# A two-block transformer kernel on one core: weight parts split in quarters beside the attentions, and the first output projection in split fp32r products

## The reference, cut to what matters

```python
# block 1
h = layernorm(concat(meta, x))                     # 528 tokens x 1024
o = concat(rmsnorm(MLA heads 0..3), rmsnorm(GQA heads 0..3))
mix = o @ w_o                                      # [512, 1024] x [1024, 1024]
h = layernorm(ALPHA * h + mix)
logits = h @ w_router; top-4 of 32 experts, softmax gates
h = layernorm(ALPHA * h + experts(h))              # 32 experts, clamped SwiGLU
# block 2
q_a, k_a, v_a, q_b, k_b, v_b, gate0, gate1 = h @ w_in_2
a = relative-bias attention, 8 heads of 64;  b = differential attention, 4 heads
h = layernorm(ALPHA * h + (g0 * (a @ w_branch_a) + g1 * (b @ w_branch_b)) @ w_out)
h = layernorm(ALPHA * h + relu(h @ w_ff1)**2 @ w_ff2)
```

## Time and profile before

| | |
|---|---|
| median of 3 runs | 2364.81 us (2363.74 to 2370.38) |
| the profiled execution | 2365.33 us, its span 2363.3 us |
| TensorE busy | 2258.0 us, 96% of the span |
| VectorE busy | 1650.4 us, 70% |
| ScalarE busy | 1208.7 us, 51% |
| mean granted TensorE clock | 0.976 |

### The profile page before, as it was taken

How to read it: one execution, slowest core, us unless ns; L and a number is a source line. 1 busy time by engine, 2 the same in 40 slices (tenths; PEclk the granted TensorE clock), 3 DMA queues, 4 the chain that set the end, 5 groups by cost and what they waited for, 6 DMA issues and landing times.

```text
span 2363.3 us, 29103 instructions
## 1 busy us (share of the span) xinstructions
PE 2258.0 (96%) x10440; PEld 1820.3 (77%) x10440; DVE 1650.4 (70%) x1575; ACT 1208.7 (51%) x1195; POOL 331.7 (14%) x274
## 2 busy tenths in 40 slices
PE   7999969999999999999999999859999999999998
PEld 4668557888888888888888888747676787888886
DVE  3636578999999999999999999742446626432434
ACT  2134325777777777777777777623334522421320
POOL 4042011211111111111211211110210010000000
PEclk9999969999999999999999999979999999999999
DMA  7010148999999999999999999653121133222220
GB/s 270 1 55 22 39 152 339 396 390 382 380 394 375 382 393 375 383 393 376 386 386 378 388 389 375 240 195 107 45 79 37 57 122 117 98 107 100 78 107 36
DMA packets 141297, 550.85 MB, mean 233 GB/s; under 512 B 11456, under 2 KB 12608, under 8 KB 124272
## 3 DMA queue, kind: packets, MB, share of 16 engines
q1 hardware_dynamic: 128048, 505.70, 55.4%
q0 software_dynamic: 11024, 39.98, 6.6%
q10 hardware_dynamic: 2160, 4.28, 0.5%
HBM read 523.71 MB, written 26.21 MB: 233 GB/s over the span
## 4 chain that ended last, share of the span: by engine, by line
PE 78%; DVE 3%; ACT 2%; issue 1%; DMA 1%; POOL 0%; DVEq 0%; ACTq 0%; POOLq 0%
PE PS L365 74%; PE PS L680 1%; PE PS L674 1%; ACT ring_parts L1472 1%; ACT act L1546 0%; DVE act L1660 0%; DVE st L1633 0%; DVE act L1665 0%; PE PS L876 0%; PE PS L790 0%; DVE small L2161 0%; DMA acc_d<-act,to_c 0%; DMA act<-acc_d 0%; DVE ring_parts L2083 0%; DMA act<-h_d,tl_c 0%
## 5 line engine op out<-in xcount | busy, mean ns | idle before, releaser
L365 PE MATMUL PS<-act_parts 128*128 128x512 f32 (+1 forms) x3324 | 1043.0, 394 | 16.3 <-DVE act_parts L1983 7.7
L1832 DVE TENSOR_TENSOR low<-ring,act_parts 128x2048 fp32r<-128x2048 f32 x396 | 886.1, 2290 | 37.1 <-ACT act_parts L1367 37.1
L365 PEld LDWEIGHTS PS<-act_parts 128*128 128x128 f32 x3324 | 625.6, 189 | 145.5 <-issue 15.9
L1367 ACT ACTIVATE act_parts<-ring 128x2048 fp32r<-128x2048 f32 x396 | 729.8, 1913 | 11.9 <-PE PS L365 8.1
L365 PE MATMUL PS<-low,act_parts 128*128 128x512 f32 x1584 | 618.7, 391 | 0.0
L365 PE MATMUL PS<-act_parts,ring_parts 128*128 128x512 f32 (+1 forms) x1280 | 376.2, 385 | 0.3 <-DVE act_parts L2201 0.3
L365 PEld LDWEIGHTS PS<-low,act_parts 128*128 128x128 f32 x1584 | 298.6, 189 | 60.5
L2083 DVE TENSOR_TENSOR ring_parts<-ring,ring_parts 128x4096 fp32r<-128x4096 f32 x30 | 132.7, 4425 | 219.1 <-ACT ring_parts L1472 219.0
L365 PEld LDWEIGHTS PS<-act_parts,ring_parts 128*128 128x128 f32 x1280 | 239.1, 191 | 59.6 <-issue 12.7
L365 PE MATMUL PS<-ring_parts,act_parts 128*128 128x512 f32 x1088 | 261.8, 393 | 2.1 <-DVE act_parts L2233 2.1
L365 PEld LDWEIGHTS PS<-ring_parts,act_parts 128*128 128x128 f32 x1088 | 205.0, 189 | 47.7 <-issue 4.3
(11 more groups left out here) (244 smaller groups left out, 1667.8 us busy)
## 6 DMA issues: line engine op xcount, KB each, us to landing
ring<-w_gate_up SPq DMA_DIRECT2D x264, 1024.0 KB, 8.6
ring<-w_down SPq DMA_DIRECT2D x132, 1024.0 KB, 7.8
ring<-w_ff SPq DMA_DIRECT2D x16, 2048.0 KB, 7.7
ring<-w_in SPq DMA_DIRECT2D x12, 2048.0 KB, 9.8
ring<-w_o SPq DMA_DIRECT2D x1, 4096.0 KB, 24.6
ring<-w_out SPq DMA_DIRECT2D x2, 2048.0 KB, 8.2
acc_d<-ring POOLq DMA_DIRECT2D x5, 512.0 KB, 3.3
act<-x SPq DMA_DIRECT2D x4, 512.0 KB, 5.5
```

Of the source, the lines that this page charges most:

```text
L365: return eng.matmul(o, lhsT, rhs, start=first, stop=last, **kw)
L1367: A_(W1hi[c % CS], W1[c], ACT.Copy).then_inc(sem["high"], 1)
L1832: tt(W1lo[c], W1[c], W1hi[c % CS].bitcast(F32), ALU.subtract).then_inc(sem["low"], 1)
```

## The change

1. In block 2, `split_piece(n, m)` splits a quarter (1024 columns) of a slot. Slots 4, 5, 6 get their quarters in units 0..3, 6..9 and 11..14 of the first attention on ScalarE (one unit later on VectorE), slots 7 and 8 in units 0..3 and 8..11 of the second. The whole-part splits of slots 4 to 8 go.
2. At the seam, the last unit's attend_a(15) moves behind scores_b(0) and beside(24), out_a(15) on ScalarE behind probs_b(0), and VectorE's masked(0) no longer waits for the last output of the first attention. At the end, attend_b(15) takes PSUM bank 6, and take_b(15) stands between two halves of heads_low(0).
3. In block 1, the projection is made from split operands: 192 fp32r matmuls for 64 float32 ones. ScalarE writes high parts of w_o times the gains (eight of 128x1024) and of the transposed heads (eight of 128x512), VectorE the eight low parts of w_o; its `take_heads` subtracts where it multiplied. The new parts lie where chunks 1 to 3 of expert 0 have their high parts, so these three move behind the projection's last matmul, on ScalarE and on VectorE.

```diff
+PIECES = 4
+SPLIT_A = ((4, 0), (5, 6), (6, 11))
+SPLIT_B = ((7, 0), (8, 8))
+WO_AT = (18, 20, 22, 23, 24, 26, 28, 30)
 # TensorE: project(g, t)
                     for k in range(4 * g, 4 * g + 4):
-                        ins = mm(PS[:, b, :], oT[:, k, t * P:(t + 1) * P], w_o_s[:, k, hf * 512:(hf + 1) * 512],
-                                 k == 4 * g, k == 4 * g + 3)
+                        if t == 0 and hf == 0:
+                            eng.wait_ge(*past("wo_low", k + 1))
+                        mm(PS[:, b, :], oThi[:, k, rows], w_o_hi[k][:, cols], k == 4 * g, False)
+                        mm(PS[:, b, :], oThi[:, k, rows], w_o_lo[:, k, cols], False, False)
+                        ins = mm(PS[:, b, :], oTlo[g][:, k - 4 * g, rows], w_o_hi[k][:, cols], False, k == 4 * g + 3)
...
 # TensorE: seam and end
-            for q in range(UA + 2):
+            for q in range(UA + 1):
...
-                if q >= 2:
+                if 2 <= q <= UA:
                     attend_a(q - 2)
...
-                b = next_bank(6)
+                if u == 0:
+                    eng.wait_ge(*past("vb2_out", 4))
+                b = next_bank(6) if u < UB - 1 else 6
...
+                if u == 0:
+                    attend_a(UA - 1)
 # ScalarE: first attentions of block 1
+                if 18 <= u < 22:
+                    turned_heads(0, u - 18)
+                if u in WO_AT:
+                    w_o_high(WO_AT.index(u))
...
-            for c in range(4):
-                chunk_high(0, c, first=True)
+            chunk_high(0, 0, first=True)
...
-            for c in range(4, CS):
+            eng.wait_ge(*past("mix_psum", 16))
+            for c in range(1, CS):
                 chunk_high(0, c, first=True)
 # ScalarE: block 2
+            def split_piece(n, m):
+                cols = slice(m * SW // PIECES, (m + 1) * SW // PIECES)
+                if m == 0:
+                    eng.wait_ge(*past(f"slot{n % NW}_in", 16 * (n // NW + 1)))
+                    eng.wait_ge(*past(*slot_used(n - NH)))
+                A_(W2hi[n % NH][:, cols], W2[n % NW][:, cols], ACT.Copy).then_inc(signal("w_high"), 1)
...
-                split_weights(c + 2)
+                if c == 1:
+                    split_weights(3)
...
-                    if n == 7 or n == 15:
-                        split_weights(5 + n // 8)
-            split_weights(7)
+                for n, at in SPLIT_A:
+                    if at <= q < at + PIECES:
+                        split_piece(n, q - at)
 # VectorE
             def take_heads(g, t):
...
-                tt(oT[:, 4 * g:4 * g + 4, t * P:(t + 1) * P], four(bank_of("oT_psum", n)), gains, ALU.mult).then_inc(
-                    signal("oT_out"), 1)
+                eng.wait_ge(*past("oT_hi", n))
+                tt(oTlo[g][:, :, rows], four(bank_of("oT_psum", n)), oThi[:, 4 * g:4 * g + 4, rows].bitcast(F32),
+                   ALU.subtract).then_inc(signal("oT_out"), 1)
+            def w_o_low(k):
+                eng.wait_ge(*past("wo_high", k + 1))
+                stt(w_o_lo[:, k, :], w_o_s[:, k, :], gq[:, 5 + k:6 + k], w_o_hi[k].bitcast(F32), ALU.mult,
+                    ALU.subtract).then_inc(signal("wo_low"), 1)
...
+                if u - 1 in WO_AT:
+                    w_o_low(WO_AT.index(u - 1))
...
-                else:
-                    chunk_low(0, 2 * t - 4)
-                    chunk_low(0, 2 * t - 3)
+                elif t == 2:
+                    chunk_low(0, 0)
...
+            chunk_low(0, 1)
             rows_low(0)
...
-            for c in range(4, 8):
+            for c in range(2, 8):
                 chunk_low(0, c)
...
-            for n in range(1, 5):
+            for n in range(1, 4):
                 split_weights(n)
...
-                if q in (5, 10):
-                    split_weights(5 + q // 10)
-            split_weights(7)
+                for n, at in SPLIT_A:
+                    if at < q <= at + PIECES:
+                        split_piece(n, q - at - 1)
...
-                if u == 0:
-                    eng.wait_ge(*past("oa_out", 2 * UA))
-                if u >= 2:
-                    eng.wait_ge(*past("expb", 2 * u - 2))
+                eng.wait_ge(*(past("expb", 2 * u - 2) if u >= 2 else past("proba", 2 * (UA - 1 + u))))
...
+                if u == UB:
+                    heads_low(0, range(2))
                 if 1 <= u <= UB:
                     take_b(u - 1)
-                if u == 8:
-                    split_weights(8)
+                for n, at in SPLIT_B:
+                    if at < u <= at + PIECES:
+                        split_piece(n, u - at - 1)
                 if u == UB:
-                    heads_low(0)
+                    heads_low(0, range(2, NT))
```

More of the change, by code:

```diff
@@ L194, in build @@
         w_in_s = ring[:, 0:KD * ZCOLS].rearrange("p (k c) -> p k c", k=KD)
-        oT = ring[:, 8192:8192 + KD * S].rearrange("p (k s) -> p k s", k=KD)
+        oThi = ring_parts[:, 8192:8192 + KD * S].rearrange("p (k s) -> p k s", k=KD)
+        oTlo = [part(9216, 4, S), part(22528, 4, S)]
         wqb = ring[:, 20480:22016].rearrange("p (k c) -> p k c", k=2)
@@ L198, in build @@
         w_o_s = ring[:, 12288:20480].rearrange("p (k c) -> p k c", k=KD)
+        w_o_lo = ring_parts[:, 12288:20480].rearrange("p (k c) -> p k c", k=KD)
+        w_o_hi = [part(at, D) for at in (5120, 6144, 7168, 8192, 14528, 15552, 18368, 19392)]
         H1 = ring[:, 20480:24576].rearrange("p (t d) -> p t d", t=NT)
@@ L592, in project @@
                 eng.wait_ge(*past("oT_out", NT * g + t + 1))
+                rows = slice(t * P, (t + 1) * P)
                 for hf in range(2):
-                    n = 8 * g + 2 * t + hf
+                    n, cols = 8 * g + 2 * t + hf, slice(hf * 512, (hf + 1) * 512)
                     b = next_bank()
@@ L1336, in heads_std, with turned_heads, w_o_high @@
                    bias=EPS_1).then_inc(signal("o_std"), 1)
+            def turned_heads(g, t):
+                n = NT * g + t + 1
+                eng.wait_ge(*past("oT_psum", n))
+                A_(oThi[:, 4 * g:4 * g + 4, t * P:(t + 1) * P], four(bank_of("oT_psum", n)), ACT.Copy).then_inc(
+                    signal("oT_hi"), 1)
+            def w_o_high(k):
+                A_(w_o_hi[k], w_o_s[:, k, :], ACT.Copy, scale=gq[:, 5 + k:6 + k]).then_inc(signal("wo_high"), 1)
             U = (HM + HG) * NT
@@ L1351, in _ @@
             heads_std(1)
+            for t in range(NT):
+                turned_heads(1, t)
             eng.wait_ge(*past("angles", 1))
@@ L1569, in _ @@
                     probs_b(u)
+                if u == 0:
+                    out_a(UA - 1)
+                if u == UB:
+                    heads_high(0)
                 if u >= 2:
                     square_b(u - 2)
-                if u == UB:
-                    heads_high(0)
+                for n, at in SPLIT_B:
+                    if at <= u < at + PIECES:
+                        split_piece(n, u - at)
                 if u < UB and u % 2:
@@ L1796, in take_heads @@
             def take_heads(g, t):
-                n = NT * g + t + 1
-                gains = gq[:, 5 + 4 * g:9 + 4 * g].rearrange("p (j o) -> p j o", o=1).to_broadcast([P, 4, P])
-                eng.wait_ge(*past("oT_psum", n))
-                tt(oT[:, 4 * g:4 * g + 4, t * P:(t + 1) * P], four(bank_of("oT_psum", n)), gains, ALU.mult).then_inc(
-                    signal("oT_out"), 1)
+                n, rows = NT * g + t + 1, slice(t * P, (t + 1) * P)
+                eng.wait_ge(*past("oT_hi", n))
[5 more added lines that the diff above has]
+                    ALU.subtract).then_inc(signal("wo_low"), 1)
             U = (HM + HG) * NT
@@ L2080, in split_weights, with split_piece @@
             def split_weights(n):
-                eng.wait_ge(*past("w_high", n + 1))
-                tt(W2lo[n % NW], W2[n % NW], W2hi[n % NH].bitcast(F32), ALU.subtract).then_inc(signal("w_low"), 1)
+                eng.wait_ge(*past("w_high", PIECES * (n + 1)))
+                tt(W2lo[n % NW], W2[n % NW], W2hi[n % NH].bitcast(F32), ALU.subtract).then_inc(
+                    signal("w_low", PIECES), PIECES)
+            def split_piece(n, m):
+                cols = slice(m * SW // PIECES, (m + 1) * SW // PIECES)
+                eng.wait_ge(*past("w_high", PIECES * n + m + 1))
+                tt(W2lo[n % NW][:, cols], W2[n % NW][:, cols], W2hi[n % NH][:, cols].bitcast(F32), ALU.subtract).then_inc(
+                    signal("w_low"), 1)
             def low(tag, XT, hi, tiles=range(NT)):
@@ L2195, in scale_heads, with heads_low @@
                        ALU.mult).then_inc(signal("ob_out"), 1)
-            def heads_low(g):
-                for t in range(NT):
+            def heads_low(g, tiles=range(NT)):
+                for t in tiles:
                     rows = o2_rows(t, g)
```

17 lines of the change are left out of this document (9 added, 8 removed).

## The result

The changed kernel takes 2340.41 us (median of 4 runs, 2338.53 to 2343.33); the kernel before, run beside it, 2364.89 us (4 runs, 2363.74 to 2370.38). The ratio is 0.9894, 95% interval 0.9882 to 0.9906. The profiled execution took 2340.29 us, its span is 2338.5 us. Forecast were 2338.5 us, range 2330 to 2350.

A forecast was written before the change was run, and what follows sets the result against it. The prediction took TensorE's time (matmuls, idle gaps, slow clock) to bound the kernel. Savings of 6.4 + 6.1 + 1.3 + 8.3 + 4.2 = 26.3 us from 2365.33 gave 2339.0, or 2338.5 against the median; range 2330 to 2350.

The forecast's parts named there:

- Block 2, first attention: Block 2's first attention: TensorE's gaps and slow clock behind them go with quarters; 6.4 + 6.1 + 1.3 us saved.
- The three gaps: TensorE's idle gaps of 4.92, 4.60 and 1.28 us in block 2's first attention, all forecast to go.
- Between the two lies at least one half product: First attention: 2.7 us of half product between VectorE's quarter and the next maximum's scores hides the quarter's 1.2 us.
- Seam, second attention, end: From take_a(15) to branch a in block 2: VectorE's sum rules, its earlier start saves 8.3 us.
- if TensorE's sum ruled, 9.7: Upper bound for seam to branch a: 9.7 us saved if TensorE's work, not VectorE's, set the time.
- TensorE's own sum: Second attention: from scores_b(0) at 1771.4, 4 x 18.11 plus 2.0 and 1.9 us, ending at 1847.7.
- Block 1, matmuls: Block 1's output projection: three fp32r products replace two-record float32 ones, 11.6 us less 1.0, so 10.6 saved.
- the 1.0 us taken off for VectorE: Projection's second half: deduction for jitter of a VectorE-TensorE tie at 8.1 us a tile and VectorE's late last-tile start.
- Block 1, what it adds: Block 1's attention loop: added w_o parts and head copies cost 1.9 us; bounds 0 and 9.8.
- waits for VectorE anyway: Block 1's loop, units 19 and 21 with take_heads: TensorE already waits, so both w_o_low overruns show, 0.9 us.
- Block 1, the moved chunks: Routing behind block 1's projection: ScalarE's five chunk copies delay the gates' exponentials; VectorE waits 4.5 us.
- The rival of the free gates: Block 1's routing: gates don't hold the chain, the 4.5 us come back, total 2334 us; chance 0.12.

The follow-up runs named there:

- e3: Changed kernel with whole parts in place of quarters, VectorE still splitting one unit after ScalarE; 2341.61 us, ratio 0.9880 to the kernel before.
- e12: Changed kernel with VectorE's quarters in the same unit as ScalarE's, not one unit later; 2339.95 us, ratio 0.9887 to the kernel before.
- e7: Changed kernel with whole parts in place of quarters and VectorE's split in the same unit as ScalarE's; 2354.57 us, ratio 0.9954 to the kernel before.
- e6: Changed kernel with VectorE's second-attention quarters between masked(u) and mix_b(u), in its wait for ScalarE, not behind take_b; 2335.76 us, ratio 0.9868.
- e8: Changed kernel with the seam's order undone: attend_a(15), out_a(15) ahead of scores_b(0), masked(0) waiting for the last outputs; 2343.66 us, ratio 0.9907.
- e4: Changed kernel with the gates' exponentials on ScalarE ahead of the high parts of chunks 4 and 5; 2336.04 us, ratio 0.9859 to the kernel before.
- e5: The changed kernel timed again with no edit, on another chip; 2341.10 us, ratio 0.9891 to the kernel before.
- e2: Kernel before with only the edits of block 2, block 1 as it was; 2346.25 us, ratio 0.9903 to the kernel before.

## Why the prediction was right, and where its steps were not

**Block 2, first attention: 13.8 forecast, 12.4 measured.** The three gaps went and the clock stood at 1.00, so the amounts held. Two steps under them did not. The first, "Between the two lies at least one half product", misses that the half product can itself be the reader of the quarter: slot 5's last quarter released one with 1.59 us of waiting. With it the stretch would have been 14.0 shorter, as forecast. The second is the reason: I credited the size of a quarter. e3 shows that the unit between ScalarE's part and VectorE's does it alone, e12 that the size does it alone, and e7, with neither, gives 7.8 us back in the first attention and 8.5 in the second against the changed kernel. What had made the gaps was the sum of two things, VectorE's wait in order behind ScalarE's part and its own 4.42 us; to take away either is enough. The diff did both at once, and my reading of the earlier trace rows took in VectorE's 4.42 us and not the wait in its brackets.

**Seam, second attention, end: 8.3 forecast, 6.35 measured.** VectorE did rule: it waited once for TensorE, early (2.57 us at 1759.36), then for ScalarE alone, and e6, whose second attention is 5.0 us shorter, bears it out. From the end of take_a(15) to the end of mix_b(15) it took 77.95 us (1753.93 to 1831.88), forecast 77.0. Behind it, to branch a, were 4.3 us and not 3.3: the gap of 0.86 at 1836.21 is TensorE waiting for ob_raw(15), since branch a's first product wants bank 6, which the change gave to attend_b(15). The forecast had that move only as a gain. The seam's own order is worth 2.6 us by time (e8), the size of the quarters some 4 in the trace of the second attention (86.98 against 82.86, e3). The order at the end was not undone alone; what it is worth stays open. The bound "if TensorE's sum ruled, 9.7" was too tight: e6 takes 78.47 us from take_a(15) to branch a (1751.51 to 1829.98), 11.4 less than before. TensorE's own sum was put too high, 74.4 us from scores_b(0) to turn_heads(0) where e6 has 71.98.

**Block 1, matmuls: 10.6 forecast, 11.2 measured.** TensorE was busy from 250.70 to 302.58 with no gap in its rows; the 1.0 us taken off for VectorE was 0.6 too much.

**Block 1, what it adds: 1.9 forecast, 1.4 measured**, with the two waits (0.20 + 0.64) behind the parts in units 19 and 21, as forecast. That TensorE "waits for VectorE anyway" there was true of one of the two before (0.34 us). ScalarE's parts of w_o took 1.14 us and not 1.06. The Trainium skill ("ScalarE: Activation LUTs", section on what ACT_TABLE_LOAD costs) says that each operand given as a column of one value a partition adds some 93 ns, and w_o_high has such a scale. The trace roughly agrees: by the groups it is 1142 less 1058, 84 ns. It lies beside other work here.

**Block 1, the moved chunks: 4.5 forecast, 4.2 measured** (a wait of 4.08 us), and e4 takes 3.6 of it back. The rival of the free gates was wrong by its own test. In the rest of the routing 0.5 us came free that I had not counted. Block 1 gave 6.1, forecast 4.2.

**The sum.** Forecast were 13.8 + 8.3 + 4.2 = 26.3 us from the profiled execution's 2365.33; the new one took 2340.29, 25.0 less. The misses are -1.4, -1.95 and +1.9, so the total is nearer than its terms, by luck in part; and the cause that I gave for the largest term was one of two, each enough alone. One reading was off and carried no term: the low slices of the earlier trace rows are 26 and 27, not 27 and 28.

## What to carry to other kernels

Where two engines prepare a piece one after the other in fixed queues, look first at what the second one waits in front of it: a stage of distance between them can be worth as much as cutting the piece, and costs nothing per instruction. Where an engine's sum is the bound, its waits for a third engine are the place for inserted work; the same 8 quarters, moved a few instructions within their unit, were worth 5 us. And when a buffer or a bank is renamed to free one waiter, ask who reads that name next.

## What the runs showed of the hardware

**VectorE and GpSimd hold each other up.** A quarter takes 1.2 us, and so it does in all 20 of the changed kernel. In e12 it often meets GpSimd's additions of two SBUF tiles, and both rows grow. Timelines of e12, VectorE and GpSimd:

```profile
1653.06 1.91 DVE L2138 TENSOR_TENSOR ring_parts<-ring,ring_parts 128x1024 fp32r<-128x1024 f32 x1 [0.61 <-ACT ring_parts L1510]
...
1662.15 2.16 DVE L2138 TENSOR_TENSOR ring_parts<-ring,ring_parts 128x1024 fp32r<-128x1024 f32 x1 [0.36 <-ACT ring_parts L1510]
```
```profile
1652.59 1.30 POOL L2506 TENSOR_TENSOR act<-act 128x512 f32<-128x512 f32 x1 [7.67 <-DVE act L2201]
1653.84 2.29 POOL L2503 TENSOR_TENSOR act<-act 128x512 f32<-128x512 f32 x1
```

The quarter begins at 1653.06 while GpSimd works until 1653.89; 1653.89 less 1653.06 is 0.83, and 0.83 + 1.2 is close to its 1.91. It ends at 1654.97; GpSimd's next row begins at 1653.84 and takes 2.29 where 1.29 is usual, the 1.1 us until then and its own 1.29. The quarter at 1662.15 meets GpSimd for 1.07 us and takes 2.16. Each sum of overlap and usual length is 0.1 to 0.2 us above its row, so the rows fit taking turns, the second held until nearly the end of the first. The Trainium skill ("SBUF — State Buffer", section on who interferes with whom) states that a VectorE instruction with two inputs in SBUF contends with a GpSimd one that reads SBUF, and that the shared ports are an exclusive lock. This trace agrees, with 1.91 and 2.16 us for 1.2. In the changed kernel it is GpSimd that waits (2.14 us at 1654.70, beside the quarter at 1654.47), and no engine's wait in that attention is put down to GpSimd.

**The same gap, another clock.** The changed kernel and e5 are the same program and have the same gap in the first attention, 1.59 and 1.58 us. In the 10 us around it the granted clock was 1.00 in the changed kernel (first line) and 0.83 in e5 (second):

```profile
1712.00:1722.00 10.00, 8.41 (x43) 6.32 (x40) 4.66 (x7) 2.17 (x6) 3.39 (x2) 1.00 0.52 198
...
1712.00:1722.00 10.00, 8.42 (x31) 6.38 (x30) 4.15 (x5) 1.67 (x5) 3.36 (x2) 0.83 0.47 179
```

The first attention is 117.31 us long in e5, 115.72 in the changed kernel. e2, e4, e6 and e8 have the gap too, with first attentions of 115.7 us (e8, cut elsewhere, with clock 1.00 in the same window): one execution of six lost its clock there. So a gap of this size may or may not cost as much again, and a single profile settles differences of 1.5 us between two attentions only if the clock is read with them.

**Stretches without an edit move too.** The 528-column exponential stood between 145.68 and 148.42 us in the profiles of this study, and the stretch of the experts took 1285.7 to 1287.8 us.
